# A streaming encoder step on one core: the up projection of both MLPs by seven block products

## What is computed

```python
def sqrelu_mlp(h, w_up, w_down):
    return jnp.square(jax.nn.relu(h @ w_up)) @ w_down
...
        xp = xp + sqrelu_mlp(rms_norm(xp, mlp_norm_g[i]), mlp_w_up[i], mlp_w_down[i])
        xs = xs + sqrelu_mlp(rms_norm(xs, mlp_norm_g[i]), mlp_w_up[i], mlp_w_down[i])
```

## Time and profile before

| | |
|---|---|
| median of 3 runs | 1467.84 us (1467.72 to 1468.32) |
| profiled execution, span | 1466.9 us |
| PE busy | 1458.1 us, 99% |
| DVE, POOL, ACT busy | 825.7, 704.1, 618.7 us |
| TensorE clock granted | full throughout |

### The profile page before, as it was taken

The page is one execution under the profiler, slowest core; times in us unless marked ns, Lnnn a source line. Parts: engine busy times, 40 slices in busy tenths (PEclk is TensorE's granted clock), DMA queues, the critical chain, the costliest instruction groups (busy, mean ns, idle before and its releaser), DMA issues.

```text
span 1466.9 us, 29051 instructions
## 1 busy us (share of the span) xinstructions
PE 1458.1 (99%) x10548; PEld 1376.3 (94%) x10548; DVE 825.7 (56%) x1499; ACT 618.7 (42%) x1234; POOL 704.1 (48%) x482
## 2 busy tenths in 40 slices
PE   9999999999999999999999999999999999999999
PEld 7889999999999999999998778787999999999999
DVE  5006716755653635636777676867556537356365
ACT  4423200123534434434637585766135344344352
POOL 8554455443363453553787052452433644535434
PEclk9999999999999999999999999999999999999999
DMA  7222232221143131231343010101221332312312
GB/s 256 85 85 73 76 107 75 68 85 59 44 130 99 60 114 57 86 114 57 115 153 92 30 44 16 43 18 40 78 67 44 123 97 68 114 57 86 115 57 93
DMA packets 36528, 120.32 MB, mean 82 GB/s; under 512 B 6056, under 2 KB 6760, under 8 KB 36208
## 3 DMA queue, kind: packets, MB, share of 16 engines
q1 hardware_dynamic: 32320, 111.83, 24.5%
q10 hardware_dynamic: 4144, 7.65, 1.7%
HBM read 115.91 MB, written 3.55 MB: 81 GB/s over the span
## 4 chain that ended last, share of the span: by engine, by line
PE 48%; DVE 3%; issue 1%; ACT 1%; DVEq 0%
PE ps L749 8%; PE ps L751 8%; PE ps L750 8%; PE ps L910 5%; PE ps L912 5%; PE ps L911 5%; PE ps L1190 2%; PE ps L1007 2%; PE ps L1130 1%; PE ps L1133 1%; PE ps L1012 1%; PE ps L1055 1%; PE ps L1102 1%; DVE lat L1572 1%; PE ps L1141 1%
## 5 line engine op out<-in xcount | busy, mean ns | idle before, releaser
L749 PE MATMUL ps<-h_hi,w_hi 128*128 128x288 f32 x1280 | 380.6, 297 | 0.0
L750 PE MATMUL ps<-h_lo,w_hi 128*128 128x288 f32 x1280 | 377.5, 295 | 0.0
L751 PE MATMUL ps<-h_hi,w_lo 128*128 128x288 f32 x1280 | 376.3, 294 | 0.0
L663 POOL TENSOR_TENSOR w_lo<-raw,w_hi 128x512 fp32r<-128x512 f32 x128 | 171.8, 1352 | 213.8 <-ACT w_hi L1904 213.8
L910 PE MATMUL ps<-op_hi,w_hi 128*128 128x288 f32 x896 | 265.5, 296 | 1.2 <-DVE x L1485 1.2
L911 PE MATMUL ps<-op_lo,w_hi 128*128 128x288 f32 x896 | 264.3, 295 | 0.0
L912 PE MATMUL ps<-op_hi,w_lo 128*128 128x288 f32 x896 | 263.4, 294 | 0.0
L751 PEld LDWEIGHTS ps<-h_hi,w_lo 128*128 128x128 f32 x1280 | 241.1, 188 | 0.0
L749 PEld LDWEIGHTS ps<-h_hi,w_hi 128*128 128x128 f32 x1280 | 239.8, 187 | 1.2
L750 PEld LDWEIGHTS ps<-h_lo,w_hi 128*128 128x128 f32 x1280 | 240.3, 188 | 0.0
L647 POOL TENSOR_TENSOR w_lo<-raw,w_hi 128x1024 fp32r<-128x1024 f32 x60 | 144.2, 2408 | 183.8 <-ACT w_hi L1896 183.8
(11 more groups left out here) (214 smaller groups left out, 2729.3 us busy)
## 6 DMA issues: line engine op xcount, KB each, us to landing
raw<-stream SPq DMA_DIRECT2D x207, 512.0 KB, 3.6
x<-xt SPq DMA_DIRECT2D x8, 288.0 KB, 6.9
out_x<-x ACTq DMA_DIRECT2D x8, 288.0 KB, 2.2
b_bc<-bs ACTq DMA_DIRECT2D x2, 512.0 KB, 6.4
cache_raw<-cache_ct ACTq DMA_DIRECT2D x1, 1024.0 KB, 6.0
v_out<-sgu_grow ACTq DMA_DIRECT2D x1, 512.0 KB, 4.8
ws_sb<-ws ACTq DMA_DIRECT2D x2, 256.0 KB, 4.9
out_v<-v_out ACTq DMA_DIRECT2D x1, 512.0 KB, 4.5
```

The source lines that it names most:

```text
L663: nc.gpsimd.tensor_tensor(block_of(w_lo, b), factor(i, b), block_of(w_hi, b).bitcast(F32), ALU.subtract).then_inc(split_lo, 1)
L749: nc.tensor.matmul(out, l_hi, r_hi, start=first, stop=False)
L750: nc.tensor.matmul(out, l_hi, r_lo, start=False, stop=False)
L751: return nc.tensor.matmul(out, l_lo, r_hi, start=False, stop=last)
```

## The change

The up half is done by seven products too. A quarter is now eight pairs n = 0 to 7: n = 0 to 3 are up, n = 4 to 7 down. Every pair has the same seven weight factors, casts and low parts, and one order of products (`product_order`). The first product of a pair, A11, is done at the end of the pair before it in the up half.

- The operand of the up half is h by blocks: four copies (x_hi_four, x_lo_four: B11, B21, B22 and T1 or T4 among seven operands) and three sums (x_hi_sums, x_lo_sums, x_lo_last), made once per MLP in `project_to_mlp` and `operands_to_mlp`.
- The sums of products of an up pair are formed in three PSUM banks: ACT copies a bank in between (`copy_first`, `keep_sum`), DVE adds (`add_u4`, `add_c22`). DVE clips (`clip_c11`, `clip_c22`, `clip_banks`), and two of four hidden blocks stay in their banks, where ACT squares them (`square_banks`). The four sums for the down half (`operand_sum`) read one SBUF operand and one bank.
- ACT casts operands from banks (`cast_banks`) and from hb (`cast_sums`, `cast_hidden`); POOL makes the low parts of those in hb (`low_hidden`), DVE the others (`low_banks`).
- SP loads two units at a time throughout, when the five POOL low parts of the pair that had the slots are made (`lows_of`).
- The statistics of the norm use other banks, and their steps stand between the first products.

ACT's queue. First an up tile pair of before, then up pair n = 1 of after (`lift` is L2205, with its wait for raw_loaded on the row ahead; `cast_sums` is L2296; L2208 is a bank copy; L2198 casts a weight factor).

POOL has two operand low parts per up pair that it did not have; the first waits for `cast_sums`. The diff, cut to the queues named above and PE's:

```diff
+def product_order():
+    order = [(0, A11)]
+    for n in range(PAIRS):
+        order += [(n, f) for f in (S1, S2, A12, S3, S4, A22)]
+        if n + 1 < PAIRS:
+            order.append((n + 1, A11))
+    for n in range(PAIRS, NPAIRS):
+        order += [(n, f) for f in (A11, A12, S1, S2, A22, S4, S3)]
+    return order
...
+            def pairs(mlp, q, unit0, last):
+                for n in range(NPAIRS - 2 if last else NPAIRS):
+                    sp.wait_ge(w_low_set, q * Q_LOW + (mlp * 4 * Q_LOW + lows_of(n)))
+                    for j in (2 * n + 4, 2 * n + 5):
+                        sp.dma_start(raw[:, j % SLOTS, :], stream[q * 16 + (unit0 + j)]).then_inc(raw_loaded[j % SLOTS], 16)
...
+            def quarter(mlp, q, last=False, next_s=None):
+                low_block(mlp, q, 1, A11)
+                for n in range(PAIRS):
+                    if n:
+                        low_hidden(mlp, q, n - 1, 3 * n, slice(5, 7), slice(2, 4))
+                    low_block(mlp, q, n + 1, A12)
+                    low_block(mlp, q, n + 1, S3)
+                    low_block(mlp, q, n + 1, S4)
+                    low_hidden(mlp, q, n, 3 * n + 1, slice(3, 5), slice(0, 2))
+                    low_block(mlp, q, n + 1, A22)
+                    if n + 1 < PAIRS:
+                        low_block(mlp, q, n + 2, A11)
+                for n in range(PAIRS, NPAIRS):
+                    if i == 0:
+                        low_hidden(mlp, q, PAIRS - 1, 3 * PAIRS + 1, slice(5, 6), slice(2, 3))
+                    if not last or n + 1 < NPAIRS:
+                        for f in (A11, A12, A22, S4, S3):
+                            low_block(mlp, q, n + 1, f)
...
+                        weights(q, n, S3)
+                        copied(q, n, 2)
+                            product(n, S3)
+                        weights(q, n, S4)
+                        read(q, "u4", n)
+                        product(n, S4)
+                        weights(q, n, A22)
+                        copied(q, n, 3)
+                        product(n, A22)
...
+                def first_down(q):
+                    n = PAIRS
+                    weights(q, n, A11)
+                    operand(q, PAIRS - 1)
+                    operand_pool(q, 2 * PAIRS - 3)
+                    product(n, A11, before_last=lambda: operand_pool(q, 2 * PAIRS - 1))
...
+                        cast_next(q, n, A11)
+                        cast_next(q, n, S1)
+                        if n:
+                            cast_banks(q, n - 1, 4, slice(0, 3), ps[:, B:B + 3, 0:TH])
+                        keep_sum(q, n, 2)
+                        cast_next(q, n, S2)
+                        lift(mlp, q, n + 2, unit0)
+                        cast_next(q, n, A12)
+                        if n:
+                            cast_sums(q, n - 1, 4)
+                        if opening and n == 0:
+                            norm_take(spread_n)
+                        keep_sum(q, n, 3)
+                        cast_next(q, n, S3)
+                        square_hidden(q, n)
+                        cast_next(q, n, S4)
+                        cast_hidden(q, n)
+                        cast_next(q, n, A22)
+                        square_banks(q, n)
```

More of the change, by code:

```diff
@@ new lines, with prod_count, made_count, cast_count @@
+PRODUCTS = product_order()
+Q_PROD = len(PRODUCTS)
+Q_LOW, Q_DVE_LOW = len(ON_POOL) * NPAIRS, len(ON_DVE) * NPAIRS
+def prod_count(n, f):
+    return PRODUCTS.index((n, f)) + 1
+def made_count(n, f, among):
+    whole = sum(g in among for _, g in PRODUCTS)
+    before = n - 1 if n else NPAIRS - 1
+    upto = sum(g in among for _, g in PRODUCTS[:prod_count(before, f)])
+    return len(among) + upto - (0 if n else whole)
+def cast_count(n, f):
+    return made_count(n, f, range(FACTORS))
+def low_count(n, f):
+    return made_count(n, f, ON_POOL if f in ON_POOL else ON_DVE)
@@ new lines, in lows_of, with read_count @@
+def lows_of(n):
+    return max(low_count(n, f) for f in ON_POOL)
+DOWN_ADDS = (A11, A12, S1, S2, A22, S4, S3)
+READS = []
+for _n in range(PAIRS):
+    READS += [(what, _n) for what in ("c11", "u4", "c22", "z22", "ab")]
+for _n in range(PAIRS, NPAIRS):
+    READS += [(_f, _n) for _f in DOWN_ADDS]
+Q_READ = len(READS)
+COPIES = [(0, 1)]
+for _n in range(PAIRS):
+    COPIES += [(_n, 2), (_n, 3)] + ([(_n + 1, 1)] if _n + 1 < PAIRS else [])
+Q_COPY = len(COPIES)
+def read_count(what, n):
+    return READS.index((what, n)) + 1
@@ L591, in _ @@
             for q in range(4):
[L592 removed]
+                pairs(1, q, U_MLP1, q == 3)
         @block.gpsimd
@@ L674, in _, with mlp_lows @@
+            def mlp_lows(mlp, next_s):
+                for f in (A11, A12, A22, S4, S3):
+                    low_block(mlp, 0, 0, f)
+                with pool.Fori(0, 3, 1) as q:
+                    quarter(mlp, q)
+                quarter(mlp, 3, True, next_s)
+            mlp_lows(0, 2)
+            for j in range(SLOTS):
+                low_unit(j)
             with pool.Fori(U_IN // SLOTS + 1, U_GRP // SLOTS + 1, 1) as i:
@@ new lines, in lift, with bank_copy @@
+            def lift(mlp, q, n, unit0):
+                slot = 2 * n % SLOTS + 1
+                act.wait_ge(raw_loaded[slot], q * 64 + loads_of(unit0 + 2 * n))
+                if n:
+                    act.wait_ge(low_set, q * Q_DVE_LOW + (mlp * 4 * Q_DVE_LOW + low_count(n - 1, S1)))
+                nc.scalar.copy(ps[:, S1_BANK, :], raw[:, slot, 0:512]).then_inc(lifted, 1)
+            def bank_copy(dst, bank):
+                nc.scalar.copy(dst, ps[:, bank, 0:TH]).then_inc(bank_copied, 1)
@@ L2148, in _weight_stream @@
         units += _feature_major(sgu_in[:, half * D:(half + 1) * D], 0, range(8))
-        units += _feature_major(sgu_out, half * D, range(8))
+        units += _feature_major(sgu_out, half * D, range(8) if half == 0 else ORDER8)
     def mlp(layer):
@@ L2168, in _weight_stream @@
         units += _units((both, 2, 512))
-    units += _feature_major(wo, 0, range(8))
+    units += _feature_major(wo, 0, ORDER8)
     units += mlp(1)
```

924 lines of the change are left out of this document (579 added, 345 removed).

## The result

The changed kernel takes 1540.17 us (median of 4 runs, 1537.37 to 1542.57), the kernel before 1467.78 in the same comparison (1467.14 to 1468.32). The ratio is 1.0492, with a 95% interval of 1.0477 to 1.0506: slower by 4.9%. The forecast was 1530, with a range of 1495 to 1568.

The account below looks back on a forecast made before the run. PE was taken to bound the kernel, busy 1458.1 of 1466.9 us. 1466.9 - 51.2 (matmuls) + 108 (round trip) + 5.8 (way in) = 1529.5, plus 0.9 for the median: 1530 us, range 1495 to 1568.

Parts of the forecast that it names:

- The gain of 51.2 us: PE's list: 48 fewer matmuls per quarter, 384 in eight quarters, at 0.1333 us each, all on the path.
- The round trip: Up pairs, lift to lift through ACT, POOL and loads: 15.15 us against PE's 11.2; 13.5 per quarter, +108 in eight.
- the landing: Last part of the trip, from POOL's end to the lift that waits for both loads: 5.4 us.
- the last quarter of the first down product: PE waits there for low_hidden(3), which POOL ends 8.5 us after the lift; PE is there at 4.9: 3.6 us.
- The clock: Idle time halves PE's clock; only behind each quarter's last wait would about 1.6 us be lost: 13, time 1543, chance 0.2.
- The way in: Start of both MLPs: operand chain, first clip and extra bank-setting matmuls +7.6 us, less 1.8 in first quarters: +5.8.
- the 0.9 that the first one saves: First quarter of each MLP: PE's slower start lets the loads catch up by 0.9 us, -1.8 together.
- 1.7: Way into an MLP: last low part behind the norm's statistics; PE covers 6.6 of about 8.3 us, leaving 1.7.
- 1.85: Way into an MLP: first clip needs rms_bc, which ACT takes and DVE uses twice, while PE has half a product: 1.85 us.
- The way out: End of MLP0, casts in another order: put at 0; a queue out of step would cost about 2.4 us.
- the loads were not in time (1424): Rival that loads come in time: lifts do not wait, up pairs run at 11.2 us, time 1424, faster by 3%; chance 0.09.
- the handovers between PE and DVE: Rival: DVE's clip and add before S4 bind, 0.75 us lost in each of 32 pairs, time 1448; chance 0.05.

Follow-up runs that it names:

- the late lift: Changed kernel with ACT's lift moved behind the cast of S4 and DVE's two first sums behind clip_c22 and clip_banks: 1460.61 us, ratio 0.9947 to the kernel before.

## Why the prediction was right, and where it was not

**The gain of 51.2 us** was right as a count (384 matmuls) and as a time. With the waits removed a quarter takes 90.3 us against 96.00, 5.7 of the 6.4 us.

**The round trip** carried the forecast, and it is shown: breaking it brings back 80 us, cutting it in two places shortens it by 1.0 and 1.3 us, and the cuts add. Its three terms were 1.80, 7.95 and 5.4 us and measured 1.79, 7.8 and 4.84 (median). So 15.15 was 0.7 too long, with most of the error in the landing: 5.4 was the middle of four cases of 4.8 to 6.9 us in other stretches. A steady quarter takes 102.2 to 102.6 us, marker to marker (411.68, 514.31, 616.56, 718.79), where the forecast had 96 - 6.4 + 13.5 = 103.1.

**Where PE feels it** was right: at A22 of pairs 1 to 3, 2.06 us after the lift (forecast 2.1), and at the last quarter of the first down product, 3.22 us (3.6). Pair 1 waits 0.8 to 1.2 us in the undisturbed quarters, where the forecast had 2.0. The named idle times of pairs 2 and 3 (2.93 and 1.67) are shorter than the 3.95 of the forecast, although the pairs take 14.4 and 14.6 us, since PE then works slower between the waits.

**The clock** was weighed as a loss of 13 us behind the last waits of the eight quarters, with a chance of 0.2, and left out of the 1530. It was there: 1.5 us in each of eight quarters, 12 us. The idea that a slow PE inside the trip costs nothing held. So a quarter's loss of 12.8 us, near the forecast's 13.5, is 11.3 of waits and late pairs and 1.5 of low clock. The waits were put 2.2 too high and the clock at nothing, and over eight quarters these two errors (-17.8 and +12) nearly cancel. That the quarters came out so close is in part luck, and of the forecast's two numbers 1543 names what happened better than 1530. The Trainium skill (TensorE: Matmul & The Clock Gate, Part 1) says that idle time halves the clock. The trace agrees at the stretches of 0.55 to 0.60, with one limit: waits of 1.9 us lowered it in five of the eight quarters with the late lift and not in the other three. The waits of 3.2 us in the changed kernel lowered it in all eight.

**The way in** failed. The forecast had 7.6 us for both MLPs. A quarter loses 102.37 - 89.6 = 12.77 us as a mean of three marker intervals. MLP0's +31.5 less the -25.6 of its matmuls is 57.1. Four quarters at 12.77 less the 0.9 that the first one saves by the forecast make 50.2, so the way in is 6.9 us. The same sum for MLP1, with 7.1 us for the standstills (below), gives 8.3. Together that is 15.2, twice the 7.6, if each first quarter did save its 0.9. The trace bears the saving out in part in MLP0, where pair 1 waits 0.47 us, and not in MLP1, where it waits 1.82. With that counted as it is, a way in costs some 6.6 us and the two first quarters together save nothing. Two terms are missing in the working: ACT's copy of the bank stood behind two operations of 576 (1.57 us), and the clock fell behind the waits, in MLP0 to 0.75 and 0.86 for 18 us. The step put down as "1.7" (x_lo_last behind the statistics) measured 1.47, and "1.85" at the first clip measured 1.38.

**The way out** was put at 0, and a queue that gets out of step at 2.4. It cost 3.2 us, because DVE's statistics were late behind the cache's low parts. The named risk was the right one, but its chance was set too low.

**The standstills of DVE** were in no step: 7.0 and 6.1 us. MLP1's markers stand at 1180.14, 1285.77, 1391.98 and 1494.29, so two of its quarters take 105.6 and 106.2 us where the third takes 102.3 and MLP0's 102.4 as a mean: 7.1 us on the path. They can't be read from the kernel before, where no such idle time stands.

**The sum.** The span of 1540.8 is 11.3 over the 1529.5 of the forecast: +7.6 for the ways in and first quarters (13.4 against 5.8), +3.2 for the way out, +7.1 for the standstills, -5.8 for the quarters (8 x 12.77 against 8 x 13.5, the clock's 12 us included), and -0.8 ahead of MLP0. The ways in are what is left over in this sum, so it closes by construction. The rivals fell: the loads were not in time (1424), and the handovers between PE and DVE never bound, since in the runs without the trip up pairs take 11.2 us outside the standstills.

## What to carry to other kernels

When a change takes work off the engine that bounds, follow one round of every buffer through all queues and compare its length with the new, shorter round of that engine. Busy shares under 63% said nothing against 14.5 us of chain for 11.2 us of work. An engine's queue order is part of that chain: one operation moved further down ScalarE's queue, with VectorE's sums moved behind it, was worth 80 us. And where a chain closes on itself, cut it in two places one at a time and then together. Cuts that add speak for one chain, and cuts that don't point to a second bound. A total that fits is no proof of its terms: here the waits were too long by nearly what the clock was too short.

## What the runs showed of the hardware

- A loop's jump can cost VectorE 6 to 7 us. It happened at both jumps of MLP1's loop in nine kernels and at neither of MLP0's, with the same body, and it went away when the loop was written out. VectorE went on 1.7 to 1.8 us after the second of two packets of an instruction queue that came 4.0 to 5.1 us apart. Transfers of 1.05 MB were under way at that moment, and their part in it is open.
- A wait of 1.9 us of TensorE was followed by a lower clock (0.60 and 0.55 in two stretches of 2 us) in five of eight quarters with the late lift. A wait of 3.2 us was in all eight of the changed kernel. Each such fall cost 1.5 us: 300 matmuls took 41.6 us instead of 40.1. Twenty small matmuls into unused columns kept the clock up.
- From POOL's end to the lift that waits for the second of two loads of 512 KB it took 4.84 us as the median of 24 (4.73 to 5.66), and 3.76 when this load was issued first.
